# A two-block network with attention, scan mixers and a top-2 expert layer: FFN inputs and first weights split in halves, expert result gated on its way to be turned, nine and nine modulation chunks

## What is computed

```python
# first block, layer i: modulation of x and of the context from w_ada (1024 x 6144)
sh1, sc1, g1, sh2, sc2, g2 = adaln(c, ada_w, ada_b)
h = modulate(x, n_mix, sh1, sc1)
o, oc = mixer(h, hc, ...)        # 0: pool + grouped-query attention over context and own keys
x = x + g1 * o                   # 1: latent attention (8 heads) + neighbourhood attention (8 heads)
x = x + g2 * swiglu(modulate(x, n_ffn, sh2, sc2), wg, wu, wd)
# attention, for every head and block of 128 queries
s = einsum("bqhgd,bkhd->bhgqk", q_blk, k) * scale
o = einsum("bhgqk,bkhd->bqhgd", softmax(s), v)
# swiglu; 2816 wide in the first block, 3584 in the second, in each expert too
(silu(h @ wg) * (h @ wu)) @ wd
# second block, last layer: router, two best of 8 experts for each token
x = x + g2 * sum_over_e(gate[t, e] * expert_e(h[t]))
out = rmsnorm(x, final)
```

## Time and profile before

| | before |
|---|---|
| runs | 2815.39, 2817.74, 2825.89 us |
| median | 2817.74 us |
| the profiled execution | 2819.95 us, span of its engines 2818.2 us |
| PE busy | 2599.6 us, 92% of the span |
| DVE busy | 1952.9 us, 69% |
| ACT busy | 1426.6 us, 51% |
| HBM read | 671.79 MB, mean 239 GB/s |
| the slices inside the expert loop | PE busy 9 tenths or more in each, 376 to 393 GB/s |

### The profile page before, as it was taken

How to read it: one execution, slowest core, us unless ns; L and a number is a source line. 1 busy time by engine, 2 the same in 40 slices (tenths; PEclk the granted TensorE clock), 3 DMA queues, 4 the chain that set the end, 5 groups by cost and what they waited for, 6 DMA issues and landing times. The chain is left out here.

```text
span 2818.2 us, 58097 instructions
## 1 busy us (share of the span) xinstructions
PE 2599.6 (92%) x22990; PEld 1969.5 (70%) x22990; DVE 1952.9 (69%) x2634; ACT 1426.6 (51%) x1733; POOL 14.9 (1%) x12
## 2 busy tenths in 40 slices
PE   6978899999887889998899998889999999999997
PEld 4735677676754457767667767668888888888885
DVE  3366455555535665555655555679999999999997
ACT  3145444443321544444254444267776776777764
POOL 0000000000200000000000000000000000000000
PEclk9989999999887899999899999889999999999999
DMA  7340555554375046545465545439999999999994
GB/s 283 125 177 23 193 205 201 215 201 156 126 274 222 1 152 223 200 167 204 149 240 201 201 158 192 149 133 396 395 396 378 378 391 377 393 381 376 392 379 169
DMA packets 121211, 674.36 MB, mean 239 GB/s; under 512 B 13488, under 2 KB 13968, under 8 KB 67088
## 3 DMA queue, kind: packets, MB, share of 16 engines
q1 hardware_dynamic: 120032, 664.47, 62.5%
q10 hardware_dynamic: 1072, 8.42, 0.8%
HBM read 671.79 MB, written 1.05 MB: 239 GB/s over the span
## 5 line engine op out<-in xcount | busy, mean ns | idle before, releaser
L933 PE MATMUL ps<-projected,normed_or_mix 128*128 128x256 bf16 x1504 | 411.5, 274 | 7.3 <-issue 7.3
L934 PE MATMUL ps<-projected,normed_or_mix 128*128 128x256 bf16 x1504 | 411.5, 274 | 0.0
L1172 PE MATMUL ps<-projected,turned 128*128 (+1 forms) x1792 | 303.1, 219 | 0.5 <-DVE turned L1284 0.5
L1172 PE MATMUL ps<-projected,normed_or_mix 128*128 (+1 forms) x1792 | 303.1, 219 | 0.4 <-DVE normed_or_mix L1284 0.4
L1173 PE MATMUL ps<-projected,turned 128*128 (+1 forms) x1792 | 303.1, 219 | 0.0
L1174 PE MATMUL ps<-projected,turned 128*128 (+1 forms) x1792 | 303.1, 219 | 0.0
L1173 PE MATMUL ps<-projected,normed_or_mix 128*128 (+1 forms) x1792 | 303.1, 219 | 0.0
L1174 PE MATMUL ps<-projected,normed_or_mix 128*128 (+1 forms) x1792 | 303.1, 219 | 0.0
L1289 DVE TENSOR_TENSOR aux<-weights,aux 128x1024 bf16<-128x1024 f32 x224 | 273.2, 1220 | 0.4 <-ACT aux L1246 0.2
L1284 DVE TENSOR_TENSOR normed_or_mix<-weights,normed_or_mix 128x2048 bf16<-128x2048 f32 x112 | 256.1, 2287 | 6.3 <-ACT normed_or_mix L1240 6.3
L1284 DVE TENSOR_TENSOR turned<-weights,turned 128x2048 bf16<-128x2048 f32 x112 | 256.2, 2288 | 3.4 <-ACT turned L1240 3.4
(11 more groups left out here) (381 smaller groups left out, 5944.4 us busy)
## 6 DMA issues: line engine op xcount, KB each, us to landing
weights<-moe SPq DMA_DIRECT2D x224, 1024.0 KB, 7.6
weights<-moe SPq DMA_DIRECT2D x224, 512.0 KB, 5.8
weights<-l_ffn SPq DMA_DIRECT2D x66, 1024.0 KB, 5.0
weights<-ada SPq DMA_DIRECT2D x64, 1024.0 KB, 5.6
weights<-l_ffn SPq DMA_DIRECT2D x66, 512.0 KB, 5.5
weights<-ada SPq DMA_DIRECT2D x64, 512.0 KB, 6.1
weights<-ffn SPq DMA_DIRECT2D x28, 1024.0 KB, 5.0
weights<-w_in SPq DMA_DIRECT2D x24, 948.0 KB, 4.7
```

Of the source, the lines that this page charges most:

```text
L933: pe.matmul(o, hi, h_hi(k), start=(k == 0), stop=False)
L934: pe.matmul(o, hi, h_lo(k), start=False, stop=False)
L1172: pe.matmul(o, hi[:, t], xh, start=(k == 0), stop=False)
```

## The change

1. In the dense FFNs ACT and DVE split the input `h` in two halves, then the first chunk's weights in a gate part and an up part. PE's first product waits for both `h_lo` halves and the gate part alone, and takes the up part's wait in the middle. `ada_kept` is no longer waited for ahead of it.
2. In the expert layer's tail the copy out of PSUM multiplies by the gate, one scalar for each partition in every 128x256 piece: DVE takes pieces 0 to 3, ACT 4 to 7, and PE turns them as they come. DVE then only adds.
3. The two routing blocks are one. The positions and selection matrices come ahead of the gate arithmetic, the matrices in two halves with a signal each. PE runs the hi gather three results ahead of the lo gather, with a wait of its own for each; the copies of lo results are shared, even ones ACT, odd ones DVE. The first expert weights are cast and split at this block's start, and the first products come ahead of the turns of `put`. PE gets eight zero products after the counts (`zero_products(pe, 8, 1)`).
4. In `attention` the turns of the first pair go to banks 4, 5, 6 (`turn_bank`) and don't wait for each other. The probabilities are handled one step later than before, and ACT does `keep_turn` ahead of `exp`.
5. The two modulation batches of 11 and 7 chunks are 9 and 9.

```diff
-    planned("ada", 11, 22)
+    planned("ada", 9, 22)
     planned("l1_uq", 2)
     planned("l1_ukv", 3)
-    planned("ada", 7, 33)
+    planned("ada", 9, 31)
...
-        pe.wait_ge(front_used.sem, n + (place.n + 1))
+        if by_half:
+            pe.wait_ge(S.w_lo.sem, S.w_lo.at(1))
+        else:
+            pe.wait_ge(front_used.sem, n + (place.n + 1))
         pe.wait_ge(S.act_done.sem, n + S.act_done.at(1))
         for w in range(2):
+            if by_half and w:
+                pe.wait_ge(front_used.sem, place.n + 1)
...
-            act.activation(h_hi, h, ACT.Copy).then_inc(S.hop_d.sem, 1)
-            cast_hi(act, 0, 0, 0)
+            for half in halves:
+                act.activation(h_hi[:, half, :], h[:, half, :], ACT.Copy).then_inc(S.h_hi.sem, 1)
+            if gates is None:
+                act.wait_ge(front_in[place.n % SLOTS].sem, 16 * (place.n // SLOTS + 1))
+                act.activation(gu[0][0][:, 0:D], RING[:, place.n % SLOTS, 0:D], ACT.Copy).then_inc(S.w_hi.sem, 1)
+                act.activation(gu[0][0][:, D:2 * D], RING[:, place.n % SLOTS, D:2 * D],
+                               ACT.Copy).then_inc(S.hi_gu.sem, 1)
...
+            act.wait_ge(expert_out.sem, 1)
+            for k in range(4, KD):
+                act.activation(gated(k)[0], gated(k)[1], ACT.Copy, scale=gate_col(k)).then_inc(S.ht_odd.sem, 1)
...
-            dve.tensor_copy(HT[:, 0:4, :], PS[:, 0:4, :]).then_inc(expert_out.sem, 1)
-            dve.wait_ge(expert_out.sem, 3)
+            for k in range(4):
+                dve.tensor_scalar(gated(k)[0], gated(k)[1], gate_col(k), None, ALU.mult).then_inc(S.ht_kept.sem, 1)
             for b in range(2):
+                dve.wait_ge(expert_out.sem, b + 2)
                 for h in range(2):
-                    t = AUX[:, (2 * b + h) * 512:(2 * b + h + 1) * 512]
-                    dve_step(dve, dve.tensor_tensor(t, PS[:, 4 + 2 * b + h, :], GB[:, h * 512:(h + 1) * 512], ALU.mult))
                     xo = X[:, b, h * 512:(h + 1) * 512]
-                    dve.tensor_tensor(xo, xo, t, ALU.add).then_inc(S.tail_added.sem, 1)
+                    dve.tensor_tensor(xo, xo, PS[:, 4 + 2 * b + h, :], ALU.add).then_inc(S.tail_added.sem, 1)
...
-                        if g >= 1:
+                        if g >= upto[0]:
                             pe.wait_ge(S.kq_kept.sem, S.kq_kept.at(g))
...
-                    if 1 <= t <= n:
-                        turn_p(t - 1, 0)
+                    if 2 <= t <= n + 1:
+                        turn_p(t - 2, 0)
...
-                    if t >= 2 and t - 2 in weighs:
-                        weigh(t - 2)
+                    if t >= 3 and t - 3 in weighs:
+                        weigh(t - 3)
...
-                for t in range(n + 3):
+                for t in range(n + 4):
+                    if t >= 4 and t - 4 in weighs:
+                        keep_out(t - 4)
                     if t < n:
                         top_of(t, 0)
                         top_of(t, 1)
-                    if t >= 3 and t - 3 in weighs:
-                        keep_out(t - 3)
-                    if t < n:
-                        weight(t, 0)
-                        weight(t, 1)
+                    if 1 <= t <= n:
+                        weight(t - 1, 0)
+                        weight(t - 1, 1)
...
-                for t in range(n + 1):
-                    if t < n:
-                        exp(t, 0)
-                        keep_turn(2 * t)
-                    if t >= 1:
-                        copy_p(t - 1, 0)
...
+                for t in range(n + 2):
+                    for i in range(2):
+                        if t < n:
+                            keep_turn(2 * t + i)
+                            exp(t, i)
+                        if t >= 2:
+                            copy_p(t - 2, i)
...
+                zero_products(pe, 8, 1)
...
+                for q in range(2 * KD + 3):
+                    if q < 2 * KD:
+                        gather(q, 0)
+                    if q >= 3:
+                        gather(q - 3, 1)
```

More of the change, by code:

```diff
@@ L1143, in ffn @@
             sg.done(beside)
-        S.hop_d.done(2)
+        for sg in (S.h_hi, S.h_lo):
+            sg.done(2)
+        for sg in (S.w_hi, S.w_lo):
+            sg.done(1)
         S.bank_done.done(3)
@@ L1499, in _ @@
                 turn_slot(-1)
-                for t in range(n + 2):
+                for t in range(n + 3):
                     if t < n:
```

184 lines of the change are left out of this document (105 added, 79 removed).

## The result

The changed kernel takes 2783.06 us (median of four runs, 2781.0 to 2788.55) against 2821.12 us for the kernel before, run beside it: a ratio of 0.9876, with a 95% interval of 0.9862 to 0.9889. The forecast was 2775 in a range of 2760 to 2793. So the total was right, 38 us where 43 were forecast. Its parts were not: two of five terms came out at little more than half and at five times their size, and the errors went against each other. Between the two profiled executions the attentions gave 9 us less than forecast and the routing 1.4 less, while the modulation chunks gave 4.6 us more and code that nobody edited 2.4 more. That the total landed so near is in part luck.

What follows compares the result with a forecast made beforehand. PE is busy nearly all the time; in layer 0's attention PE and DVE wait for each other. Terms -9.2, -6.9, -4.7, -21, -1.1 sum to -42.9: 2819.95 to 2777.0, less 2.2 for the median, 2775 us; range 2760 to 2793.

Steps and rivals of the forecast that it cites:

- FFN starts: Dense FFNs: earlier first products 5.9 us, clock staying up behind the third and fourth 3.3; -9.2 us (-5.5 to -9.5).
- Tail: Expert layer's tail: gated pieces shared by DVE and ACT, PE following them; -4.7 us (-4 to -5.2).
- Routing: Routing block: earlier and shorter gather, next work at 1865.35 where it was 1872.20; -6.9 us (-4.5 to -8.5).
- at 1848.5, 4.6 us sooner: Routing: PE's gather starts at 1848.5, as counts and half the selection matrices are ready by about 1848.4.
- Attentions: Three attentions, steps handled one later: layer 0 -12.5, MLA -4, NA -4.5; sum -21 us (-10 to -26).
- some six tenths of it, as above: MLA: that share of PE's 6.35 us idle time goes, as in layer 0; -4 us (-1.5 to -5).
- rival (a): Attentions gain little, the cycle of score, turn and exponent sets their pace; -10 for the three, 2786 us; chance 0.15.
- Modulation chunks: Two norm stages: first 6.1 us shorter, second 5.0 longer; net -1.1 us (-3.6 to 0).
- +5.0: Second norm stage: nine chunks end at 915.1 with PE at 1.2 GHz, 5.0 us longer (+2.5 at full clock).
- (b): Expert loop gives the routing's gain back, as transfers set its pace; 2782 us; chance 0.04.
- (d): Slower: PE stays at 1.2 GHz in the attentions of layer 0 and MLA; 2856 us; chance 0.02.
- (e): FFN starts: PE's first product waits for something other than DVE's lo; 9 us less gain, 2784 us; chance 0.02.

Runs made afterwards that it cites:

- att_before: The changed kernel with the whole attention function of before (part 4 undone): 2796.86 us, ratio 0.9918 to the kernel before.
- att_shallow: The changed kernel with its turn banks and ACT's keep_turn first, but probabilities as early as before in all three attentions: 2786.72 us, ratio 0.9884.
- both_depths: The changed kernel with the late step and ACT's copies ahead of exponents in layer 0's attention only, probabilities early in MLA and NA: 2772.47 us, ratio 0.9837.
- ffn_filled: The changed kernel with dense FFN starts as before, plus ten more zero products ahead of PE's wait in each FFN: 2784.0 us.
- ffn_before: The changed kernel with dense FFN starts as before (part 1 undone: whole casts, PE waits for the whole lo): 2789.95 us.

## Why the prediction was right, and where it was not

**FFN starts: right, with its mechanism.** 4.69 us against the forecast 4.75, and the clock stayed up; two experiments show that it was PE's idle time. The second FFN's 0.3 us did not come (6.98 us after, 6.65 before): there PE is busy up to its first product, with rows of the modulation at a granted clock of 0.51. In att_before, att_shallow and both_depths, with 0.71 in that place, the same start took 5.5 to 5.7 us.

**Tail: right.** 4.66 us for 4.7. A gated piece took 0.475 us on ACT, less than the 0.55 of the forecast's lower bound (and more than the 0.38 of a plain copy of that size, L1584).

**Routing: 5.5 us for 6.9.** The stretch itself gave 4.3, and 1.2 came in the loop behind it, which the sum had at nothing. The step that failed is the gather's start "at 1848.5, 4.6 us sooner": it came 2.8 us sooner, 14.4 us behind the logits' start where it had been 17.2. I took logits and counts at their durations of before and had the zero products hidden "if they end before 1848.5". They ran at 1.2 GHz and did not end in time. In ffn_filled, where the clock was higher in that place, the gather started 12.44 us behind the logits' start and the routing took 29.71 us: the forecast's own numbers, at the other clock. The seven other kernels with this routing and eight zero products all took 31.9 us, and nothing in the routing differs in ffn_filled; why the clock was higher there is open. The rest of the step held: the gather took 14.3 us for 13.8.

**Attentions: 12 us for 21, the term that was mis-sized most.** In layer 0 I took 13.7 us for a pair of before and 11.6 after. The first was right: the pairs of before start 12.77, 13.45, 15.35, 13.45 and 13.45 us behind one another, 13.7 in the mean. The step that failed is the 11.6: after the change they are 12.82, 12.01, 12.49, 12.00 and 12.00, 12.3 in the mean, so a pair gained 1.4 us and not 2.1. I had left 0.8 us "for handoffs" without naming which; it is one wait, for ACT's copy out of a bank with one buffer, and ACT's order put it behind an exponent. For MLA the step that failed is "some six tenths of it, as above": a share of idle time carried over from layer 0 without looking at what PE waited for. In MLA of the kernel before, PE waited for the division of a probability once, for 0.3 us:

```profile
PE ps L1484 <- DVE probs_turned L1534: 0.3, 1, 0.3
```

There the late step gives 0.5 us between first and last score and lengthens the end by 2.4 us, which cancels the 2.2 us that the banks save at the start. I had charged the extra step to drain in layer 0 alone, against the banks' gain, and had left it out of MLA and NA. The sum lay inside my bounds (-10 to -26), near the poor one, and nearer to the price of rival (a), -10, than to the forecast. But rival (a) named the wrong reason for it: it put the limit into the exponents' cycle.

**Modulation chunks: -5.7 (-8.1 in the experiment) for -1.1.** The step that failed is the second stage's "+5.0": I had the ninth chunk's work at 1.2 GHz, 6.6 us from its rows to ACT's last copy. It took 3.9 us plus the copy's own 0.2 (885.10 to 889.18) at full clock, and the rows started 27.7 us behind the first ones, for 28.5. The stage grew by 2.0 us, less even than the +2.5 that I had for full clock; I chose by the level that the earlier trace rows showed. That level does occur: in ffn_before the same nine chunks have their last rows 28.6 us behind the first and the work behind them takes 7.25 us at a clock of 0.50, so the stage takes 5.4 us more than before the change.

```profile
859.78:895.62 35.84, 30.47 (x199) 15.09 (x199) 26.89 (x55) 10.68 (x24) 0.00 (x0) 0.64 0.85 340
```

In eight of the ten kernels with nine chunks there the stage takes 32.2 to 32.4 us. In the first stage the price of the two chunks, 6.1 us, was right. The other 1.6 of its 7.7 us came ahead of them: the ninth chunk's rows stand 29.3 us behind the first ones and not 30.9, since one chunk fewer was taken at 4.1 us, the spacing at 1.2 GHz, before the clock rose. The net, -5.7, lies outside the bounds that I gave this term (-3.6 to 0).

**The other rivals.** (b) fell: the loop passed the routing's gain on, with 1.2 us more (its slices before the change go up to 396 GB/s, and not 393). (d) fell: the mean clock in layer 0 is 0.91 for 0.93, in MLA 0.92 for 0.90, and 1.00 in the steady pair. So the swing of the clock that the prediction weighed beside (d), from the Trainium skill (TensorE: Matmul & The Clock Gate, "A second HAM failure mode: psum-queue depth-cycling"), is not seen in this kernel. (e) fell too: PE's idle time ahead of the first product of the first, third and fourth FFN went from 2.3 to 0.4 us.

## What to carry to other kernels

The worth of a software pipeline one step deeper has to be read from each call's waits. In layer 0 it took PE's wait for divided probabilities from 11.2 us (att_shallow) to 0.7 and gained 5.3 us between first and last score; in MLA 0.3 us of such waits stood there before and it gained 0.5; in NA the wait stayed and it gained nothing. The ends of MLA and NA grew by 2.4 and 1.4 us. So count the end's steps for each call, not once. After a wait is taken out, look for the buffer that is single on the same path: here it was the PSUM bank of turned probabilities, and the order of two operations on the engine that empties it was worth 4 us. And price a step of a stage at both levels of the clock before choosing one; two of the five terms, the routing and the chunks, were off for the most part by that choice.

## What the runs showed of the hardware

- An idle time of 2.3 us of PE ahead of an FFN's products was followed by a stretch at 1.2 GHz in two FFNs of the kernel before and of ffn_before (7.07 instead of 5.40 us for 48 products), and by none once it was filled with zero products or cut to 0.4 us. In the first FFN it was followed by none in either kernel.
- In the routing, keeping PE busy moved the slow stretch rather than removing it: eight zero products gave the gather 2.0 us and took 1.1 us in the loop behind it, and they delayed the gather by 0.6. Six delayed it by nothing, and the gather took 14.5 us for 14.3.
- Unedited stretches moved by 1 to 5 us from kernel to kernel with the granted clock and the landing of weights; the stretch from layer 0's modulation chunks to its attention took 36.4 to 36.8 us in three kernels (the changed one, att_before, both_depths) and 33.4 to 33.6 in all others. In the three, the work behind the last chunk's rows took 7.17 us at a granted clock of 0.50, in the others 4.66 at 1.00. A single total can't show an edit of 5 us here, and its stretch can.
